# Joining three edits in a two-block fp32 transformer kernel: latent-attention keys and rotations, the norms of block 2, and the RG-LRU gelu

## The chip, the cores and the metric

The kernel runs on one core of a Trainium2 chip, as one program and one launch. The metric is the device time of an execution in microseconds (us), lower is better; the number to forecast is the median of several executions. TensorE is called PE here, its weight loads PEld, VectorE DVE, ScalarE ACT, GpSimd POOL, and SyncE SP.

## The reference

512 tokens of width 1024 in fp32 go through two blocks of two layers each. A layer of block 1 joins three attention branches (latent attention "MLA", a dilated one, a neighbourhood one) by gates and adds a SwiGLU part. Block 2 has a retention layer and an RG-LRU layer, each followed by a SwiGLU part, with a norm before and after each part:

```python
for layer in range(DEPTH):                       # block 2
    h = rms_norm_2(x, norm_g[layer, 0])
    m = retention_mixer(...) or rglru_mixer(...)
    x = x + rms_norm_2(m, norm_g[layer, 1])
    f = swiglu_ffn(rms_norm_2(x, norm_g[layer, 2]), ...)
    x = x + rms_norm_2(f, norm_g[layer, 3])
...
# rglru_mixer
y_branch, u = jnp.split(x @ w_in, 2, axis=-1)
y_branch = jax.nn.gelu(y_branch, approximate=True)
u = conv4(u) + conv_b
r, i = sigmoid(u_blocks @ gate_w + gate_b)       # 6 blocks of 256
log_a = -LRU_C * r * softplus(-a_param)
b = sqrt(-expm1(2 * log_a)) * (i * u)
h = associative_scan(a, b)
return (h * y_branch) @ w_out
```

## The kernel before

**Products.** Activations lie transposed, 128 features by 512 tokens a tile. Each fp32 operand is split into a high part that PE takes in fast (fp32r) and a low remainder: `zh, zl` for activations, `wh, wl` for weights. A 128x128 tile of weights against a tile of activations is three matmuls of 512 columns: `wh*zh, wh*zl, wl*zh`. In the trace such a step is the rows `zh,wh`, `zl,wh`, `zh,wl`.

**Weights.** All weights lie in one tensor in the order in which PE takes them, in chunks of eight tiles. SP loads a chunk into `raw` (two buffers), ACT copies it to `wh`, DVE subtracts to `wl` (a ring of three each), and both count as "the split". Where in its own work ACT or DVE splits the next chunk is decided by `reach(mark, n)` (up to chunk n after a named point), by `ahead()`, or by a wait that needs that chunk.

**Order.** There is no scheduler: every engine's program is written out by hand, and `wait_ge`/`tell` tie them with semaphores. `claim(bank, ...)` makes PE wait until the last user of one of the eight PSUM banks has been moved out. In the attention parts PE takes units (one head's 128 queries each): transposes, scores, value products, and then some "fill" steps of other products, as many as `SLOTS` say.

**MLA (`tensor_mla`, `vector_mla`, ...).** 32 units. A unit's chain is: PE scores, DVE minimum (L1248), ACT exp, DVE reciprocal (L1088), POOL division `m_p` (L578), PE transpose, ACT and DVE split `m_pth, m_ptl`. The query of the next head is turned on DVE (`m_qf`), then split on ACT (`m_qh`) and POOL (`m_ql`). The rotations of the dilated part's first heads run in between: shuffle and sine on DVE, cosine (`b_qk<-b_qk,b_rc`) on POOL.

**Dilated and neighbourhood parts.** `b_bank`, `BV_BANK`, `gate_bank`, `proj_bank`, `c_bank` give the bank of each fill; `FILL_N` is the order of the fills in the neighbourhood part: gate g and projection p of 8 column tiles, query q and key k of the last head pairs. Gates of odd number and all q lie in bank 1. DVE moves a fill out in the unit after the one in which it ended.

**After each part of block 2 (`*_post`).** `ret`, `f20`, `lru` and `f21` are the four posts. Eight output tiles come (the last in two halves of 256 tokens), their squares are summed over features by one-column matmuls (`tensor_half`), POOL takes the root, PE spreads it over the partitions, DVE scales `mb`, DVE or POOL adds it to `x2`, and then the next part's `zh` (ACT) and `zl` (DVE) are made by halves. PE begins the next part with three tiles by halves (`halves`). The squares of the new x for its norm are ACT's, 16 of 256 tokens, and each is summed by PE with one-column matmuls (`bank<-small,mb`): after each of the eight second-half steps (`early`) and after four steps of the next tile (`late`). `f21` has no next part.

**RG-LRU (`*_lru`).** Six blocks b of two tiles: PE takes the gates' matmuls of block b and then the input products of block b+2; ACT, DVE and POOL run the recurrence, and `u_hyh, u_hyl` (`scalar_hy`, `vector_hy`) are the operands of the output product. After the gates of block 4, PE goes to output tiles 0 to 3 over inputs 0 to 7. The gelu: ACT squares `u_y` into `u_q`, ACT scales and biases it, POOL multiplies by `u_y`, ACT takes tanh, DVE multiplies.

## Time and profile before

| | us |
|---|---|
| median of 3 executions (3360.37 to 3360.75) | 3360.4 |
| the profiled execution's own time | 3354.7 |
| its span, first to last instruction | 3352.9 |
| PE busy | 3282.0 (98%) |
| DVE, ACT, POOL busy | 1783.3, 1318.1, 604.8 |

PE is busy nearly throughout, so only time in which PE waits, works at half clock, or does work that could be left out can be won. The time of a matmul in a row is longer than its spacing to the next one, since they overlap; spacings are read from the starts.

### The profile page before, as it was taken

The page shows a single profiled execution, that of the slowest core. Times are in us where ns is not written, and L with a number is a line of the kernel's source. Part 1 is how long each engine was busy: PE and PEld are TensorE (multiplying, and loading weights), DVE is VectorE, ACT ScalarE, POOL GpSimd, SP SyncE. Part 2 cuts the span into 40 slices and gives each one's busy share as a digit, 9 for nine tenths or more (in the row PEclk, how much of TensorE's full clock was granted, in tenths as well). Part 3 has the DMA queues.
Part 4 walks back from the last instruction along what each step waited for, and adds up shares of the span by engine and source line. Part 5 has one row for each costly group of instructions (what it writes and reads, how often), then busy time and mean ns, then how long its engine had stood idle before and what let it go on. Part 6 is the DMA issues. An engine that isn't in the chain of part 4 may idle for free.

```text
span 3352.9 us, 38507 instructions
## 1 busy us (share of the span) xinstructions
PE 3282.0 (98%) x15604; PEld 2722.5 (81%) x15604; DVE 1783.3 (53%) x2671; ACT 1318.1 (39%) x2025; POOL 604.8 (18%) x516
## 2 busy tenths in 40 slices
PE   8999999999999999999999999999999999999998
PEld 7787878888887887788888888888888888788887
DVE  6764565444447655755444455544444359854433
ACT  5643453333236534533332323333232248733321
POOL 1420122011003310320110021111111025521101
PEclk9999999999999999999999999999999999999999
DMA  3022223222321122222323222222232222223232
GB/s 133 32 70 76 96 90 107 95 95 94 100 90 57 58 71 78 98 95 94 101 94 105 94 79 81 90 88 76 95 100 95 98 73 88 95 65 106 96 99 82
DMA packets 84993, 295.61 MB, mean 88 GB/s; under 512 B 9424, under 2 KB 11984, under 8 KB 84816
## 3 DMA queue, kind: packets, MB, share of 16 engines
q1 hardware_dynamic: 84816, 293.15, 26.4%
q8 instruction: 123, 2.02, 0.2%
q14 instruction: 54, 0.44, 0.0%
HBM read 291.02 MB, written 2.10 MB: 87 GB/s over the span
## 4 chain that ended last, share of the span: by engine, by line
PE 83%; DVE 8%; ACT 4%; issue 2%; POOL 2%; DMA 1%; SPq 0%; POOLq 0%; DVEq 0%; ACTq 0%
PE bank L312 81%; PE bank L315 2%; DVE wl L555 2%; ACT wh L528 1%; DVE small L1248 1%; POOL u_g L575 1%; DVE u_uc L551 1%; DMA raw<-in_wts 1%; DVE m_ptl L555 1%; POOL u_q L575 0%; DVE u_h L3123 0%; ACT c_k L528 0%; ACT b_v L528 0%; POOL x L575 0%; DVE m_qf L545 0%
## 5 line engine op out<-in xcount | busy, mean ns | idle before, releaser
L555 DVE TENSOR_TENSOR wl<-raw,wh 128x1024 fp32r<-128x1024 f32 (+1 forms) x531 | 682.2, 1288 | 860.4 <-ACT wh L528 859.4
L312 PE MATMUL bank<-zh,wh 128*128 128x512 f32 (+1 forms) x2652 | 1034.3, 390 | 14.7 <-ACT zh L528 7.7
L312 PE MATMUL bank<-zl,wh 128*128 128x512 f32 (+1 forms) x2652 | 1022.7, 386 | 5.5 <-DVE zl L558 5.4
L312 PE MATMUL bank<-zh,wl 128*128 128x512 f32 (+1 forms) x2652 | 1023.2, 386 | 4.0 <-DVE wl L555 4.0
L528 ACT ACTIVATE wh<-raw 128x1024 fp32r<-128x1024 f32 (+1 forms) x531 | 556.4, 1051 | 537.8 <-PE bank L312 477.3
L312 PEld LDWEIGHTS bank<-zh,wh 128*128 128x128 f32 x2652 | 502.1, 189 | 116.0 <-ACT zh L528 8.0
L312 PEld LDWEIGHTS bank<-zh,wl 128*128 128x128 f32 x2652 | 501.8, 189 | 109.1 <-DVE wl L555 8.3
L312 PEld LDWEIGHTS bank<-zl,wh 128*128 128x128 f32 x2652 | 502.1, 189 | 102.3 <-DVE zl L558 7.6
L312 PE MATMUL bank<-f_mh,wl 128*128 128x512 f32 (+1 forms) x748 | 283.7, 379 | 1.2 <-DVE wl L555 1.2
L312 PE MATMUL bank<-f_mh,wh 128*128 128x512 f32 (+1 forms) x748 | 284.1, 380 | 0.0
L312 PE MATMUL bank<-f_ml,wh 128*128 128x512 f32 (+1 forms) x748 | 281.4, 376 | 0.0
L575 POOL TENSOR_TENSOR f_t<-f_t 128x512 f32<-128x512 f32 x88 | 113.6, 1291 | 792.6 <-DVE f_t L551 792.6
L581 POOL TENSOR_TENSOR small<-small 128x1 f32<-128x1 f32 (+3 forms) x35 | 44.3, 1265 | 965.5 <-DVE small L548 965.5
L531 ACT ACTIVATE f_t<-f_t 128x512 f32<-128x512 f32 x88 | 55.6, 632 | 293.4 <-DVE f_t L545 293.3
L312 PEld LDWEIGHTS bank<-f_mh,wl 128*128 128x128 f32 x748 | 140.4, 188 | 29.6 <-DVE wl L555 1.6
L312 PEld LDWEIGHTS bank<-f_ml,wh 128*128 128x128 f32 x748 | 140.4, 188 | 28.1
L312 PEld LDWEIGHTS bank<-f_mh,wh 128*128 128x128 f32 x748 | 140.6, 188 | 25.4
L312 PE MATMUL bank<-wh,zh 128*128 128x512 f32 (+2 forms) x384 | 145.0, 378 | 0.7 <-ACT r_r L528 0.7
L312 PE MATMUL bank<-wl,zh 128*128 128x512 f32 (+2 forms) x384 | 143.7, 374 | 1.5 <-DVE wl L555 1.5
L528 ACT ACTIVATE f_mh<-f_t 128x512 fp32r<-128x512 f32 x88 | 55.6, 632 | 227.3 <-POOL f_t L575 227.3
L312 PE MATMUL bank<-wh,zl 128*128 128x512 f32 (+2 forms) x384 | 143.9, 375 | 0.0
L545 DVE TENSOR_TENSOR f_t<-bank,rrow 128x512 f32<-128x512 f32 x88 | 60.8, 691 | 141.3 <-PE bank L312 130.6
(336 smaller groups left out, 4483.4 us busy)
## 6 DMA issues: line engine op xcount, KB each, us to landing
...
```

Source lines behind the costliest of these rows:

```text
L312: return self.e.matmul(out, l, r, start=start, stop=stop, skip_group_check=inside)
L315: return self.e.transpose(out, in_, self.m.ident)
L528: return self.e.activation(out, in_, ACT.Copy, scale=scale)
L531: return self.e.activation(out, in_, func, **kw)
L545: return self.e.tensor_tensor(out, a, b, op)
L551: return self.e.scalar_tensor_tensor(out, a, s, b, op0, op1)
L555: return self.e.tensor_tensor(out, src, b32(hi), ALU.subtract)
L575: return self.e.tensor_tensor(out, a, b, op)
L581: return self.e.tensor_tensor(out, v, self.m.negh[:, 0:n], ALU.pow)
L1248: L.e.tensor_reduce(m.mn[:, c:c + 1], m.bank[4 + i % 2], AX.X, ALU.min).then_inc(*L.tell("mn", "mla", l, i))
```

## The change

It joins edits in several places. (1) MLA: the cosine product of the six early rotations goes from POOL to DVE; each head's query is turned one unit sooner; the low parts of the values (`m_v`) are made in units 0 and 1, no longer ahead of unit 0. (2) Dilated part: the fills take banks 2, 1, 0, 1, 0, 1 and no longer 0, 1, 0, 1, 0, 1; DVE moves a projection out after the reciprocal and no longer ahead of it. (3) Neighbourhood part: the fills q3 and k3 come ahead of g2 and p2. (4) Posts: the squares for the next norm are 8 of 512 tokens at the end, DVE adds them up, and PE sums over features once, with four one-column matmuls, three tiles later; the second half of the last output tile has bank 4; scaled rows come at k = 6; splits are placed by `reach`. (5) RG-LRU: the gelu's middle is one DVE instruction in place of ACT's and POOL's; output tiles 0 to 3 take inputs 0 to 5 and then 6 and 7; `hy` of blocks 3 and 5 comes sooner; one `reach` ahead of the rows.

```diff
-BV_BANK = ((3, 4, 5, 6), (2, 1, 3, 0))
+BV_BANK = ((3, 4, 5, 6), (2, 1, 0, 3))
...
-    return (2, 7)[w] if p == 0 and g == 0 else w if p else 0
+    if p:
+        return (2, 1, 0, 1, 0, 1)[2 * g + w]
+    return 0 if g else (2, 7)[w]
...
+    if p == 0:
+        x = m.b_qk[p][2 * g + w]
+        L.tt(x, x, m.b_rc, ALU.mult).then_inc(*L.tell("ev", "cos", *n))
...
-    L.wait_ge("pl", *n)
+    if p == 0:
+        L.wait_ge("ev", "cos", *n)
+    else:
+        L.wait_ge("pl", *n)
...
+def vector_mv(L, l, t):
+    m = L.m
     vv = m.m_v.rearrange("p (t h d) -> p t h d", t=4, h=8)
-    for t in range(4):
-        L.wait_ge("hi", "mv", l, t)
-        L.lo(vv[:, t, :, 64:128], m.bank[V_BANK[t]].rearrange("p (h d) -> p h d", h=8), vv[:, t, :, 0:64]).then_inc(
-            *L.tell("lo", "mv", l, t))
-    L.ahead()
+    L.wait_ge("hi", "mv", l, t)
+    L.lo(vv[:, t, :, 64:128], m.bank[V_BANK[t]].rearrange("p (h d) -> p h d", h=8), vv[:, t, :, 0:64]).then_inc(
+        *L.tell("lo", "mv", l, t))
...
@@ scalar_mla, vector_mla, gpsimd_mla
-        if i % 4 == 2 and i < 30:
+        if i % 4 == 1 and i < 29:
             scalar_q(L, l, i // 4 + 1)
...
+        if i < 2:
+            vector_mv(L, l, 2 * i)
+            vector_mv(L, l, 2 * i + 1)
...
-        if i in B_TURN:
-            gpsimd_b(L, ("b", l, 0) + B_TURN[i])
...
-                yield from L.steps(n, 8, L.z_whole(), b_desc, w, ("cp",) + n)
+                yield from L.steps(n, 8, L.z_whole(), b_desc, b_bank(n), ("cp",) + n)
...
@@ vector_dil
             if x == "g":
                 vector_gate(L, l, 0, n)
-            else:
-                vector_proj(L, l, 0, n)
...
             vector_div(L, i, *key)
+        for x, n in at(p, i, 1) if p else ():
+            if x == "p":
+                vector_proj(L, l, 0, n)
...
-FILL_N = bb(0) + [("q", 2), ("k", 2)] + bb(1, 2) + [("q", 3), ("k", 3)] + bb(3, 4, 5, 6, 7)
+FILL_N = bb(0) + [("q", 2), ("k", 2)] + bb(1) + [("q", 3), ("k", 3)] + bb(2, 3, 4, 5, 6, 7)
...
-POST_BANK = {"ret": (0, 1, 2, 3, 4, 5, 0, 2, 3), "f20": (2, 3, 6, 7, 4, 5, 0, 1, 2), "f21": (2, 3, 6, 7, 4, 5, 0, 1, 2),
-             "lru": (4, 5, 6, 7, 0, 1, 2, 3, 2)}
+POST_BANK = {"ret": (0, 1, 2, 3, 4, 5, 0, 2, 4), "f20": (2, 3, 6, 7, 4, 5, 0, 1, 4), "f21": (2, 3, 6, 7, 4, 5, 0, 1, 4),
+             "lru": (4, 5, 6, 7, 0, 1, 2, 3, 4)}
 POST_SCALE = {"ret": 1.0, "f20": 1.0, "f21": 1.0, "lru": -0.125}
-POST_AT = {"ret": 0, "f20": 3, "f21": 3, "lru": 0}
-POST_ROWS = {"ret": 7, "f20": 9, "f21": 9, "lru": 7}
+POST_AT = {"ret": 1, "f20": 3, "f21": 3, "lru": 0}
+POST_ROWS = 6
+
+POST_EARLY = {"ret": 1, "f20": 0, "lru": 1}
...
-    sb, rb = ((6, 7), (4, 5))[h]
+    sb, rb = 6, (7, 5)[h]
...
@@ scalar_post
+    if nxt:
+        L.reach(("z2", s), POST_EARLY[s])
     for h in range(2):
         for n in range(8):
             if nxt:
-                g = m.col(nxt)
                 L.wait_ge(*x_ready(s, n, h, False))
-                L.cp(half(m.zh[n], h), half(m.x2[n], h), g[:, n:n + 1]).then_inc(*L.tell("zh", "z2", s, n, h))
-                L.fn(half(m.mb[n], h), half(m.x2[n], h), ACT.Square).then_inc(*L.tell("cp", "xsq", s, n, h))
+                L.cp(half(m.zh[n], h), half(m.x2[n], h), m.col(nxt)[:, n:n + 1]).then_inc(*L.tell("zh", "z2", s, n, h))
             if h == 0 and n == POST_AT[s]:
                 scalar_m7(L, s, 1)
                 if nxt:
                     L.reach(("z2", s), 1)
-            if nxt and h == 0 and n == POST_AT[s] + 3:
+            if nxt and h == 0 and n == POST_AT[s] + 2:
                 L.reach(("z2", s), 2)
-            if h:
-                L.ahead()
+            if nxt and h and n == 6:
+                L.reach(("z2", s), 3)
+    for n in range(8 if nxt else 0):
+        L.fn(m.mb[n], m.x2[n], ACT.Square).then_inc(*L.tell("cp", "xsq", s, n))
+        if n == 3:
+            L.reach(("z2", s), 4)
...
@@ vector_post
-        L.ts(m.mb[n], m.bank[POST_BANK[s][n]], g[:, n:n + 1], POST_SCALE[s], ALU.mult, ALU.mult).then_inc(
-            *L.tell("ev", "m", s, n))
         if n:
             if n > 1:
                 L.wait_ge("sq", "m", s, n - 1)
             L.tt(m.sqa, m.sqa, m.sqt, ALU.add).then_inc(*L.tell("sq", "m", s, n))
+        L.ts(m.mb[n], m.bank[POST_BANK[s][n]], g[:, n:n + 1], POST_SCALE[s], ALU.mult, ALU.mult).then_inc(
+            *L.tell("ev", "m", s, n))
...
+            if nxt and h == 0 and n == 2:
+                L.reach(("z2", s), POST_EARLY[s])
+            if h == 0 and n == POST_AT[s] + 2:
                 vector_m7(L, s, g, 1)
-            if h == 0 and n == POST_AT[s] + 2:
                 if nxt:
                     L.reach(("z2", s), 1)
+            if h == 0 and n == POST_AT[s] + 3:
...
+    if nxt:
+        L.reach(("z2", s), 3)
+    for n in range(1, 8 if nxt else 0):
+        if n > 1:
+            L.wait_ge("sq", "x", s, n - 1)
+        else:
+            L.wait_ge("cp", "xsq", s, 0)
+        L.wait_ge("cp", "xsq", s, n)
+        L.tt(m.mb[0], m.mb[0], m.mb[n], ALU.add).then_inc(*L.tell("sq", "x", s, n))
+        if n == 4:
+            L.reach(("z2", s), 4)
...
@@ tensor_next_stat
-    def squares(h, ns):
-        def go():
-            ps = L.claim(6, "rv", *N) if (h, ns[0]) == (0, 0) else m.bank[6]
-            for n in ns:
-                L.wait_ge("cp", "xsq", s, n, h)
-                for r in (2 * h, 2 * h + 1):
-                    new = (h, n, r) == (0, 0, 0)
-                    t = L.mm(ps[:, r:r + 1], m.mb[n][:, 128 * r:128 * r + 128], m.ones, new, new or n == 7, not new)
-            if (h, ns[-1]) == (1, 7):
-                t.then_inc(*L.tell("st", "stat", *N))
-        return go
-
-    return ({(1, k): squares(0, (k,)) for k in range(8)}, {k: squares(1, (2 * k, 2 * k + 1)) for k in range(4)}, L.spread(N))
+    def squares():
+        ps = L.claim(6, "rv", *N)
+        L.wait_ge("sq", "x", s, 7)
+        L.sums(ps, 0, m.mb[0], True).then_inc(*L.tell("st", "stat", *N))
+
+    return squares, L.spread(N)
...
@@ tensor_ffn2
-             {(0, 0): squares1, (0, 3): rows1, **early})
+             {(0, 0): squares1, (0, 4): rows1})
     n = F + (1, 1)
-    L.group([n], 8, L.z_whole(), f2_in_desc, [3], [("ev",) + n], late)
+    L.group([n], 8, L.z_whole(), f2_in_desc, [3], [("ev",) + n])
     for i in range(2, FF):
         n = [F + (w, i) for w in range(2)]
         L.group(n, 8, L.z_whole(), f2_in_desc, [f_bank(i, w) for w in range(2)], [("ev",) + x for x in n],
-                {1: rows} if i == 2 else {})
+                {0: squares, 2: rows} if i == 2 else {})
...
@@ tensor_lru
-    pair(y[0:2], y_bank, {1: rows})
+    pair(y[0:2], y_bank, {0: squares, 2: rows})
...
-            for i in (0, 2):
-                tensor_post_pair(L, "lru", i, LW, x, lru_out_desc, range(8))
+            for ks in (range(6), range(6, 8)):
+                for i in (0, 2):
+                    tensor_post_pair(L, "lru", i, LW, x, lru_out_desc, ks)
...
-    q = m.u_q[n % 2]
-    L.fn(q, m.u_y[n % 4], ACT.Square).then_inc(*L.tell("cp", "y2", n))
+    L.fn(m.u_q[n % 2], m.u_y[n % 4], ACT.Square).then_inc(*L.tell("cp", "y2", n))
+
+
+def vector_y_cube(L, n):
+    q, v = L.m.u_q[n % 2], L.m.u_y[n % 4]
     L.wait_ge("cp", "y2", n)
-    L.fn(q, q, ACT.Identity, scale=0.044715 * 0.7978845608028654, bias=m.gel).then_inc(*L.tell("cp", "y3", n))
-
-
-def gpsimd_gelu(L, n):
-    q, v = L.m.u_q[n % 2], L.m.u_y[n % 4]
-    L.wait_ge("cp", "y3", n)
-    L.tt(q, q, v, ALU.mult).then_inc(*L.tell("pl", "y3", n))
+    L.stt(q, q, 1.0 / 0.044715, v, ALU.add, ALU.mult).then_inc(*L.tell("ev", "y3", n))
 
 
 def scalar_gelu(L, n):
     q = L.m.u_q[n % 2]
-    L.wait_ge("pl", "y3", n)
-    L.fn(q, q, ACT.Tanh).then_inc(*L.tell("th", "y", n))
+    L.wait_ge("ev", "y3", n)
+    L.fn(q, q, ACT.Tanh, scale=0.044715 * 0.7978845608028654).then_inc(*L.tell("th", "y", n))
...
@@ scalar_lru
+    L.reach(("z2", "f20"), 7)
...
+        if b in (4, 6):
+            scalar_hy(L, b - 1)
         if b < 6:
             scalar_recur(L, b)
+        for n in nxt:
+            scalar_y_square(L, n)
         lru_reach(L, b, 1)
-        if b:
+        if b in (1, 2, 3, 5):
             scalar_hy(L, b - 1)
         for n in nxt:
             scalar_us(L, n)
-        lru_reach(L, b, 2)
-        for n in nxt:
-            scalar_y_square(L, n)
...
@@ vector_lru
+        if b in (4, 6):
+            vector_hy(L, b - 1)
...
+        if b == 5:
+            vector_hy(L, b - 1)
+        for n in nxt:
+            vector_y_cube(L, n)
...
```

Three places in the order of the instructions follow. PE, after the retention part: the last step of the second half of the first three tiles (256 columns), and the steps that follow (bank 3 is the fourth tile, `mb0` to `mb7` the squares of x). Before:

```order
L312 MATMUL bank2<-zh,wl1 128x256
L312 MATMUL bank6<-small,mb7 128x1 x2
L312 MATMUL bank3<-zh,wh2 128x512
L312 MATMUL bank3<-zl,wh2 128x512
L312 MATMUL bank3<-zh,wl2 128x512
L312 MATMUL bank6<-small,mb0 128x1 x2
L312 MATMUL bank6<-small,mb1 128x1 x2
```

And of the changed kernel, where the only such rows stand, one tile later (banks 4 and 5 are the third pair of tiles):

```order
L312 MATMUL bank4<-zh,wl0 128x512
L312 MATMUL bank5<-zh,wh0 128x512
L312 MATMUL bank5<-zl,wh0 128x512
L312 MATMUL bank5<-zh,wl0 128x512
L312 MATMUL bank6<-small,mb0 128x1 x4
L312 MATMUL bank4<-zh,wh0 128x512
```

Thirty-two one-column matmuls of a post have become four, and they come after one step of the third pair.

PE, neighbourhood part of layer 0, unit 5: scores, then the last two steps of projection 1 (`ybh, ybl`, bank 0), then the next fill. Before:

```order
L312 MATMUL bank5<-c_kl1,c_q10 128x256
L312 MATMUL bank0<-ybh,wh2 128x512
L312 MATMUL bank0<-ybl,wh2 128x512
L312 MATMUL bank0<-ybh,wl2 128x512
L312 MATMUL bank0<-ybh,wh2 128x512
L312 MATMUL bank0<-ybl,wh2 128x512
L312 MATMUL bank0<-ybh,wl2 128x512
L312 MATMUL bank2<-zh,wh2 128x512
```

Of the changed kernel, from the same place:

```order
L312 MATMUL bank0<-ybh,wh2 128x512
L312 MATMUL bank0<-ybl,wh2 128x512
L312 MATMUL bank0<-ybh,wl2 128x512
L312 MATMUL bank1<-zh,wh2 128x512
L312 MATMUL bank1<-zl,wh2 128x512
```

The fill behind the projection was gate 2 in bank 2 and is now q3 in bank 1, where gate 1 ended at the end of unit 4.

DVE, RG-LRU, from the scan of block 3 to the third split (`u_h` is the scan, `u_y` the input of the gelu, `u_uc` the convolution). Before:

```order
L3123 SCALAR_TENSOR_TENSOR u_h<-u_t,u_g 128x512 x2
L555 TENSOR_TENSOR wl<-raw,wh 128x1024 x2
L545 TENSOR_TENSOR u_y<-bank,rrow 128x512 x2
L551 SCALAR_TENSOR_TENSOR u_uc<-u_pad,cols,u_uc 128x512 x6
L555 TENSOR_TENSOR u_hyl<-u_h,u_hyh 128x512 x2
L555 TENSOR_TENSOR u_usl<-u_uc,u_ush 128x512 x2
L551 SCALAR_TENSOR_TENSOR u_g<-u_g,u_uc 128x512 x2
L555 TENSOR_TENSOR wl<-raw,wh 128x1024
L551 SCALAR_TENSOR_TENSOR u_t<-u_t 128x512 x4
L555 TENSOR_TENSOR wl<-raw,wh 128x1024
```

Of the changed kernel:

```order
L3143 SCALAR_TENSOR_TENSOR u_h<-u_t,u_g 128x512 x2
L555 TENSOR_TENSOR wl<-raw,wh 128x1024 x2
L545 TENSOR_TENSOR u_y<-bank,rrow 128x512 x2
L555 TENSOR_TENSOR u_hyl<-u_h,u_hyh 128x512 x2
L551 SCALAR_TENSOR_TENSOR u_uc<-u_pad,cols,u_uc 128x512 x6
L555 TENSOR_TENSOR u_usl<-u_uc,u_ush 128x512 x2
L551 SCALAR_TENSOR_TENSOR u_g<-u_g,u_uc 128x512 x2
L555 TENSOR_TENSOR wl<-raw,wh 128x1024
L551 SCALAR_TENSOR_TENSOR u_t<-u_t 128x512 x4
L551 SCALAR_TENSOR_TENSOR u_q<-u_q,u_y 128x512 x2
L555 TENSOR_TENSOR wl<-raw,wh 128x1024
```

`u_hyl` now stands ahead of the convolution, the third split stays behind both, and the cube `u_q<-u_q,u_y` is new.

## Rows read from the trace of the kernel before

**Rows 1.** Waits of PE, whole run: us in total, times, longest.

```profile
PE bank L315 <- POOL m_p L578: 7.5, 10, 1.0
...
PE bank L312 <- DVE u_hyl L555: 5.4, 1, 5.4
PE bank L312 <- DVE zl L558: 5.4, 6, 1.6
PE bank L312 <- DVE m_qf L545: 4.8, 8, 1.4
PE bank L312 <- DVE b_v L558: 3.0, 2, 1.6
PE bank L312 <- DVE c_kl L555: 3.0, 2, 1.5
PE bank L312 <- ACT wh L528: 2.9, 2, 1.5
...
PE bank L312 <- POOL m_ql L575: 2.3, 2, 1.2
PE bank L315 <- POOL b_p L578: 2.3, 2, 1.1
...
PE bank L312 <- DVE mb L548: 2.0, 1, 2.0
```

**Rows 2.** Instructions on tile mb, PE: ns min/median/max, first and last start.

```profile
L312 PE MATMUL bank<-small,mb x192: 164/250/250, 2340.6 to 2997.8; 128*128 128x1 f32 x192
```

**Rows 3.** Timeline of PE behind the retention post: start us, us, instruction.

```profile
2339.54 0.28 PE L312 MATMUL bank<-zh,wh 128*128 128x256 f32 x1
...
2340.62 0.50 PE L312 MATMUL bank<-small,mb 128*128 128x1 f32 x4
...
2342.13 0.50 PE L312 MATMUL bank<-small,mb 128*128 128x1 f32 x4
...
2352.34 0.95 PE L312 MATMUL bank<-small,mb 128*128 128x1 f32 x8
...
2353.48 0.40 PE L312 MATMUL bank<-zl,wh 128*128 128x512 f32 x1
2353.71 0.39 PE L312 MATMUL bank<-zh,wl 128*128 128x512 f32 x1
2353.95 0.95 PE L312 MATMUL bank<-small,mb 128*128 128x1 f32 x8
```

**Rows 4.** Timeline of DVE in the retention post; brackets: idle before, releaser.

```profile
2324.59 0.48 DVE L548 TENSOR_SCALAR mb<-bank,cols 128x256 f32<-128x256 f32 x1 [2.06 <-ACT rrow L531]
...
2325.32 0.48 DVE L558 SCALAR_TENSOR_TENSOR zl<-x,cols,zh 128x256 fp32r<-128x256 f32 x1
```

**Rows 5.** Windows at half clock: length, busy (count) by engine, granted clock, DMA.

```profile
184.20:187.70 3.50, 3.50 (x10) 2.71 (x10) 2.33 (x5) 0.89 (x2) 0.00 (x0) 0.51 0.22 62
2327.80:2334.70 6.90, 5.89 (x26) 5.32 (x26) 5.26 (x12) 3.23 (x7) 3.98 (x5) 0.51 0.37 122
2891.00:2897.90 6.90, 4.81 (x11) 3.80 (x12) 6.90 (x12) 4.69 (x7) 2.50 (x1) 0.51 0.00 0
```

**Rows 6.** Timeline of DVE in RG-LRU block 4.

```profile
2892.36 1.28 DVE L555 TENSOR_TENSOR u_hyl<-u_h,u_hyh 128x512 fp32r<-128x512 f32 x2
...
2895.97 1.21 DVE L555 TENSOR_TENSOR wl<-raw,wh 128x1024 fp32r<-128x1024 f32 x1
```

**Rows 7.** Timelines of POOL and DVE in RG-LRU block 1.

```profile
2807.22 7.73 POOL L575 TENSOR_TENSOR u_q<-u_q,u_y 128x512 f32<-128x512 f32 x2 [10.36 <-ACT u_q L531]
...
2815.05 1.70 DVE L551 SCALAR_TENSOR_TENSOR u_y<-u_q,u_y 128x512 f32<-128x512 f32 x1 [1.30 <-ACT u_q L531]
```

**Rows 8.** Timeline of POOL in MLA.

```profile
78.48 1.80 POOL L575 TENSOR_TENSOR b_qk<-b_qk,b_rc 128x512 f32<-128x512 f32 x1 [0.56 <-DVE m_sh L783]
```

**Rows 9.** Timelines of PE and DVE, neighbourhood part, unit 5, layer 0.

```profile
413.64 0.39 PE L312 MATMUL bank<-zh,wh 128*128 128x512 f32 x1
...
416.30 0.67 DVE L545 TENSOR_TENSOR f_g<-bank,rrow 128x512 f32<-128x512 f32 x1
```

More of the change, by code:

```diff
@@ L1256, in vector_mla @@
             L.lo(lo, f4(m.bank[turn_bank(j)]), hi).then_inc(*L.tell("lo", "pt", "mla", l, j))
-        if i % 4 == 2 and i < 30:
+        if i % 4 == 1 and i < 29:
             vector_q_turn(L, l, i // 4 + 1)
@@ L1276, in gpsimd_mla @@
             gpsimd_div(L, i - 1, m.m_p[(i - 1) % 4], "mla", l)
-        if i % 4 == 2 and i < 30:
+        if i % 4 == 1 and i < 29:
             gpsimd_q(L, l, i // 4 + 1)
-        if i in B_TURN:
-            gpsimd_b(L, ("b", l, 0) + B_TURN[i])
         if i >= 16 and i % 8 == 0:
@@ L2647, in tensor_post @@
     L.halves([("m", s, 7)], K, (by_half(x[0]), by_half(x[1])), desc, [[POST_BANK[s][7]], [POST_BANK[s][8]]],
-             [[("ev", "m7", s, h)] for h in range(2)], {(1, 2): squares, (1, POST_ROWS[s]): rows}, False)
+             [[("ev", "m7", s, h)] for h in range(2)], {(1, 2): squares, (1, POST_ROWS): rows}, False)
     L.end(("post", s), "pe")
@@ L2725, in stat @@
         L.wait_ge("st", "half", s, h)
-        L.ts(m.vtmp[:, c], m.bank[(6, 4)[h]][:, c], 1.0 / 1024, EPS, ALU.mult, ALU.add).then_inc(*L.tell("rv", "half", s, h))
+        L.ts(m.vtmp[:, c], m.bank[6][:, c], 1.0 / 1024, EPS, ALU.mult, ALU.add).then_inc(*L.tell("rv", "half", s, h))
     def z(n, h):
@@ L2745, in vector_post @@
                 z(n - 2, h)
-            if h == 0 and n == POST_AT[s] + 1:
+            if nxt and h == 0 and n == 2:
+                L.reach(("z2", s), POST_EARLY[s])
+            if h == 0 and n == POST_AT[s] + 2:
                 vector_m7(L, s, g, 1)
-            if h == 0 and n == POST_AT[s] + 2:
                 if nxt:
                     L.reach(("z2", s), 1)
+            if h == 0 and n == POST_AT[s] + 3:
                 stat(1)
@@ L2753, in vector_post @@
                 L.reach(("z2", s), 2)
-            if h:
-                L.ahead()
         if nxt:
@@ L2774, in gpsimd_post @@
                 L.tt(half(m.x2[n], h), half(m.x2[n], h), half(m.mb[n], h), ALU.add).then_inc(*L.tell("pl", "x", s, n, h))
-            if h == 0 and n == POST_AT[s] + 2:
+            if h == 0 and n == POST_AT[s] + 3:
                 rms(1)
@@ L2814, in tensor_ffn2 @@
     squares1, rows1 = tensor_half(L, prev, 1)
-    early, late, rows = tensor_next_stat(L, prev)
+    squares, rows = tensor_next_stat(L, prev)
     first = [F + wi for wi in ((0, 0), (1, 0), (0, 1))]
@@ L2899, in tensor_lru @@
     y = [("y", i) for i in range(LW)]
-    early, late, rows = tensor_next_stat(L, prev)
+    squares, rows = tensor_next_stat(L, prev)
     L.skip()
@@ L2903, in tensor_lru @@
     L.halves(u[:3], 8, L.z_by_half("z2", prev), lru_desc, [range(3)] * 2, [[("ev",) + n for n in u[:3]]] * 2,
-             {(0, 0): squares1, (0, 3): rows1, **early})
-    L.group(u[3:4], 8, L.z_whole(), lru_desc, [3], [("ev", "u", 3)], late)
+             {(0, 0): squares1, (0, 4): rows1})
+    L.group(u[3:4], 8, L.z_whole(), lru_desc, [3], [("ev", "u", 3)])
     def pair(ns, bank, extra={}):
         L.group(ns, 8, L.z_whole(), lru_desc, [bank(n[1]) for n in ns], [("ev",) + n for n in ns], extra)
-    pair(y[0:2], y_bank, {1: rows})
+    pair(y[0:2], y_bank, {0: squares, 2: rows})
     pair(y[2:4], y_bank)
@@ L3215, in vector_lru @@
     L.wait_ge("ev", "pads")
+    L.reach(("z2", "f20"), 7)
     L.wait_ge("rr", "z2", "f20")
@@ L3229, in vector_lru @@
     for n in range(2):
+        vector_y_cube(L, n)
+    for n in range(2):
         vector_gelu(L, n)
@@ L3240, in vector_lru @@
         lru_reach(L, b, 1)
-        if b:
+        if 0 < b < 4:
             vector_hy(L, b - 1)
@@ L3249, in vector_lru @@
             vector_recur(L, b)
+        if b == 5:
+            vector_hy(L, b - 1)
+        for n in nxt:
+            vector_y_cube(L, n)
         lru_reach(L, b, 3)
@@ L3262, in gpsimd_lru @@
     gpsimd_stat(L, ("z2", "f20"))
-    for n in range(2):
-        gpsimd_gelu(L, n)
     for b in range(7):
@@ L3267, in gpsimd_lru @@
             gpsimd_hv(L, b - 1)
-        if b < 5:
-            for n in (2 * b + 2, 2 * b + 3):
-                gpsimd_gelu(L, n)
         if b < 6:
```

## The prediction

> **What bounds the kernel now.** I began with the table of busy times. PE is busy 3282.0 of 3352.9 us, every other engine far less: a stretch is shorter only if PE has less to do, waits less, or works less at half clock. So I took the waits of PE [rows 1]. The reader is to see that no wait dominates: the longest are single ones (5.4 us for `u_hyl` in the RG-LRU), and most are families of ten waits of a microsecond, which recur in both layers of block 1 (`m_p`, `m_qf`, `b_v`). The ten rows sum to 38.6 us. Next I looked for work of PE that does not multiply weights: the one-column matmuls on `mb` [rows 2] and their spacing [rows 3]. Last the windows at half clock [rows 5]: in each the granted clock is 0.51, that is 1.2 GHz where 2.4 is granted elsewhere, and each stands right behind waits of PE.
>
> **The sum, part by part.** Each price is PE time.
>
> *1. Squares of the posts.* A second-half step is nine matmuls of 256 columns: from 2339.54 to 2340.62 they take 1.08 us. With a squares group between, the spacing of two groups is 2342.13 - 2340.62 = 1.51 us, so four short records cost 0.43 us. A late group: 2353.95 - 2352.34 = 1.61 us for eight records and three matmuls of 512 columns spaced 0.23 (2353.48 to 2353.71), 0.69 us: 0.92 us for eight records [rows 3]. A post has eight early and four late groups, 3.4 + 3.7 = 7.1 us. 192 records on three posts [rows 2] become 24, one group of eight a post, 0.92 us. Gain (7.1 - 0.9) x 3 = **18.6 us**. The Trainium skill ("TensorE: Matmul & The Clock Gate", section Back-to-back issue gap) gives about 60 cycles for a lone matmul of 1 to 64 columns, 25 ns at 2.4 GHz; by it 168 records would be worth 4.2 us. The rows show 0.11 us a record, and they decide.
>  What takes the squares' place lies off PE: ACT's squares are 8 of 512 for 16 of 256, DVE gets seven additions of 512 elements (0.67 us each by `f_g` [rows 9], 4.7 us), and both can lie under the fourth tile and the first step of the third pair (5.5 + 1.4 us of PE at 0.23 a matmul), which start when the second halves are done. Without that cover each late microsecond is one of PE, three times. POOL's root has two steps (2.7 us) until PE wants its rows: I cost it at nothing, 0 to 1 us a post.
>
> *2. Waits and clock in the posts.* In the retention post DVE stood 2.06 us for the second half of the last tile (`rrow`), with the first `zl` queued behind it [rows 4]: that move now stands two tiles later, so the first 1.6 us wait on `zl` should go. ACT without its 16 squares feeds `zh` sooner, which is for the other `zl` waits. The bank of the second half of the last tile is now one emptied first: the 2.0 us on `mb` goes. The first split after `f20` is now stated ahead: half of ACT `wh`'s 2.9, 1.5 us. Together 5.4 + 2.0 + 1.5 = 8.9 [rows 1]; since some waits will only shrink, **8 us** (bounds 2 and 8.9). The window at 2327.80 holds 26 matmuls in 6.90 us at 0.51 [rows 5]. Its wait for `zl` apart, 26 matmuls spaced 0.12 would be 3.1 us, so the clock costs about 2 there. Behind the RG-LRU post PE works the same way, and I put it at the same: **4 us** together (0 to 5).
>
> *3. RG-LRU.* PE waits 5.4 us for `u_hyl` of block 3, behind twelve tiles of the output product; released at 2893.0 when the first `u_hyl` ends [rows 6]. Now twelve tiles of pair 2, 3 come first, 12 x 0.69 = 8.3 us: the wait is covered. What is late next: the split behind. PE would want its `wl` at 2887.6 + 8.3 + 0.5 = 2896.4; it ended at 2895.97 + 1.21 = 2897.2 [rows 6], and ACT's two squares (1.2 us) now stand ahead of `u_ush`: about 2898.5. A new wait of 2 to 2.5 us. The half clock behind the old wait (11 matmuls in 4.81 us busy [rows 5], 2.5 at 0.23) gives 2.2 back. 5.4 + 2.2 - 2.5 = **5.1 us** (1 to 7.6). Splits ahead of the rows at the start: the other half of ACT `wh`, **1.4 us**.
>  The gelu: DVE gets 12 cubes, 0.67 us each by `f_g` again, two a block. I cost them at nothing, because DVE stood 1.30 us before the first gelu multiply for ACT's tanh [rows 7]; with the cover gone they are 8.0 us. POOL loses `u_q`, of which two took 7.73 us [rows 7], while DVE ran on. The Trainium skill ("SBUF — State Buffer", section Who interferes with whom) says that a DVE instruction with two SBUF inputs and a POOL instruction that reads SBUF exclude each other; the cubes have two such inputs, so POOL's later products may have to wait behind them as `u_q` did. No row prices this for the new order.
>
> *4. MLA.* `b_qk` on POOL takes 1.80 us [rows 8], and the next `m_p` stands behind it. Six times a layer this goes; DVE's cosine in its place delays the next minimum by 0.67, so I count half of the 7.5 us of `m_p`, 3.7. Queries one unit sooner should end nearly all of `m_qf` 4.8 and `m_ql` 2.3 [rows 1]; 5.8. Sum **9.5 us** (0 to 14.6). The values' low parts move from ahead of the first minimum to units 0 and 1: four DVE instructions of 512 elements that are wanted only by the first value product in unit 6; the cover is the fill work of PE.
>
> *5. Dilated part.* The first fill has bank 2, emptied first, not bank 0 emptied last: 3.0 us of `b_v` [rows 1], and the spell at 184.20, 10 matmuls in 3.50 us for 2.3 at 0.23, but with the last begun before its end: 1.6 us a time, two layers 3.2. **6.2 us** (3.0 to 6.2). The projection behind the reciprocal: `b_p`, **2.3 us** (0 to 2.3; the projection's bank is free 0.7 us later, under eight steps of gate).
>
> *6. Neighbourhood part.* q3 and k3 ten steps sooner end `c_kl`, +3.0 us [rows 1]. But q3 claims bank 1, where gate 1 ended in the unit before, with two steps of projection between. The next fill starts at 413.64; DVE moves gate 1 out (`f_g`) from 416.30 to 416.97 [rows 9]. Behind q3 PE's scores of unit 6 are queued, and DVE and ACT for them. New wait 3.3 us, two layers: -6.7. Sum **-3.7 us** (+3.0 to -10 with half clock behind it).
>
> Sum: 18.6 + 8 + 4 + 5.1 + 1.4 + 9.5 + 6.2 + 2.3 - 3.7 = 51.4 us. The profiled execution goes from 3354.7 to 3303.3, its span from 3352.9 to 3301.5; the median of the runs is 5.7 above the profiled one, and I keep that: 3360.4 - 51.4 = **3309.0**.
>
> **Rivals.**
> *DVE becomes what is waited for.* It gets 12 cosines, 12 cubes and 21 additions, 45 x 0.67 = 30 us. For: in MLA it is already in the chain of each unit. Against: it is 53% busy over the run. Then MLA gives nothing, the cubes cost 5, and the posts' waits give 3 of 8: 51.4 - 9.5 - 5 - 5 = 32 us, 3328.
> *All waits named go, and q3 finds its bank empty.* For: the order of DVE could shift by what the other edits free. Against: the rows of unit 5. 51.4 + 6.7 + 5 (the rest of MLA) + 2.5 = 66 us, 3295.
> *The short matmuls cost little.* The 0.43 and 0.92 us could be change-over that the remaining order has anyway. Then part 1 is worth 4.2: 37 us, 3323. Against it: 0.43 us for four and 0.92 for eight are in proportion to the number of records, not of change-overs [rows 3]. The section of the Trainium skill named in part 1 would have it so.
> *Slower.* Mechanism: a wait of 3.3 us in the neighbourhood part or the split in the RG-LRU brings a long stretch at half clock. In the first window a matmul takes 0.35 us and more for 0.23, a loss of up to 1.6 us in 3.5 [rows 5]; to turn 51 us of gain into a loss of 0.2% (6.7) it takes 58 us, some 120 us at half clock. Against: the spells are 3.5 to 6.9 us long, the one behind the wait of 5.4 us too [rows 5]. It ends at 3368.
> *No change.* The gains do not add because one chain through DVE sets the time; little speaks for it at 98% PE.
>
> **How the numbers follow.** Forecast 0.46; DVE 0.26; all waits go 0.21; short matmuls 0.03; slower 0.02; no change 0.02. The range reaches from the case of all waits gone (3295) to that of DVE (3328) and, since costs in both layers and three posts repeat, some 7 us further: 3296 to 3335. Outside lie the last two cases and about half of a further tenth on each side. A change of 0.2% (6.7 us) is about what a measurement of this kernel tells from none: faster 0.96, same 0.02, slower 0.02.
>
> **What the changed profile would show.** Right: 24 records of `bank<-small,mb`; no early groups, second-half steps spaced 1.08; no waits on `b_v`, `u_hyl`, `mb`, `c_kl`; a wait of PE for `f_g` of some 3 us in each neighbourhood part; a wait for `wl` of 2 to 2.5 us in the RG-LRU output product; fewer half-clock spells in the posts; `m_p` waits of 0.5. Wrong would be: waits of PE on `mb<-mb` sums or on the root's rows of more than 1 us a post, minima of MLA starting later against PE than now, or a family of new `wl` waits in the RG-LRU because the cubes hold the splits back.

## The result, and the profile after

| | before | after |
|---|---|---|
| median of the executions, us | 3360.6 | 3325.1 (3324.4 to 3325.5, 4 runs) |
| profiled execution, own time | 3354.7 | 3324.4 |
| span | 3352.9 | 3322.6 |
| PE busy | 3282.0 | 3257.8 |
| DVE, ACT, POOL busy | 1783.3, 1318.1, 604.8 | 1805.0, 1309.0, 561.5 |

The ratio is 0.9894 (95% interval 0.9877 to 0.9911): faster by 35 us, where 51 were forecast. The sum of the steps was made for the profiled execution, and there the gain is 30.4 us. The other 5 us are a spread of the kernel before: its times went from 3353.0 to 3362.5 us over all its executions, and the one that I read was short. (One execution of a version below, that with 64 records a post, took 4653 us at a mean granted clock of 0.65, and stands in no ratio.)

The waits of PE in the changed kernel (us in total, times, longest), beside [rows 1]:

```profile
PE bank L315 <- POOL m_p L578: 13.2, 16, 2.1
...
PE bank L312 <- DVE f_g L545: 6.3, 2, 3.1
PE bank L315 <- POOL b_p L578: 5.2, 2, 2.6
PE bank L312 <- DVE wl L555: 4.6, 6, 1.5
PE bank L315 <- DVE c_ptl L555: 3.5, 2, 1.7
PE bank L312 <- DVE zl L558: 2.9, 2, 2.1
PE bank L312 <- DVE acc L551: 2.5, 2, 1.3
PE bank L312 <- DVE m_yf L545: 2.4, 2, 1.2
...
PE bank L312 <- DVE b_v L558: 0.7, 2, 0.4
...
PE bank L312 <- DVE u_hyl L555: 0.7, 1, 0.7
```

The reader is to see two things. What was named as going did go: `m_qf`, `m_ql`, `c_kl`, `mb` and ACT `wh` are not in the list, `b_v` and `u_hyl` nearly so. And block 1 has new ones in their place: `m_p` 5.7 us more, `f_g` 6.3, `b_p` 2.9 more, `c_ptl` 3.5, `acc` 2.5, `m_yf` 1.8 more.

Apart from the records on `mb` PE takes the same steps in both kernels, so the times at which the same step starts in the two timelines give a balance by stretch (us, to some 0.2; plus is a loss):

| stretch | forecast | measured |
|---|---|---|
| MLA, layers 0 and 1 | -9.5 | -0.1, +1.8 |
| dilated part | -8.5 | +1.3, +0.4 |
| neighbourhood part | +3.7 | +2.4, +3.8 |
| three posts, splits at the RG-LRU's start included | -32.0 | -10.9, -11.6, -9.4 |
| RG-LRU up to the end of its output product | -5.1 | -8.6 |
| the rest | 0 | +0.6 |
| sum | -51.4 | -30.3 |

Block 2 gave 40.5 us where 37.1 were forecast. Block 1, which was to give 14.3, took 9.6. The windows at half clock (length, PE's work and that of the others, granted clock, DMA), beside [rows 5]:

```profile
79.50:82.90 3.40, 3.40 (x12) 2.71 (x11) 3.37 (x7) 1.18 (x4) 0.69 (x1) 0.50 0.00 0
192.10:195.50 3.40, 3.40 (x10) 2.54 (x10) 1.98 (x7) 2.21 (x4) 0.91 (x1) 0.50 0.00 0
...
2943.30:2950.10 6.80, 6.80 (x34) 6.80 (x33) 4.99 (x11) 2.04 (x4) 5.47 (x6) 0.50 0.32 117
```

The first stands behind a wait of 2.07 us on `m_p`, the second behind 2.61 us on `b_p`. There are six of 3.4 us in block 1 and this one in block 2; before there were 10 us in block 1 and 20 in block 2. The last 7 to 8 us of a run, which are at half clock in every version, are left out here and below.

### The profile page after: what moved, and what is told of

Read it like the earlier page. It is cut to its first block, busy times and chain, and to the rows that moved or that the text cites. A ratio compares the mean times of both kernels' runs of the same rounds, so it can differ in the third digit from the quotient of the medians.

```text
span 3322.6 us, 38212 instructions
## 1 busy us (share of the span) xinstructions
PE 3257.8 (98%) x15436; PEld 2702.9 (81%) x15436; DVE 1805.0 (54%) x2716; ACT 1309.0 (39%) x1989; POOL 561.5 (17%) x492
## 4 chain that ended last, share of the span: by engine, by line
PE 83%; DVE 8%; ACT 3%; issue 2%; POOL 2%; DMA 1%; SPq 0%; POOLq 0%; DVEq 0%; ACTq 0%
PE bank L312 82%; PE bank L315 2%; DVE wl L555 1%; ACT wh L528 1%; DVE small L1258 1%; POOL u_g L575 1%; DMA raw<-in_wts 1%; ACT c_k L528 1%; DVE m_ptl L555 1%; DVE u_uc L551 0%; DVE m_qf L545 0%; DVE c_kf L545 0%; DVE u_t L551 0%; DVE b_yf L545 0%; DVE c_ptl L555 0%
```

## The experiments

Spans come from one profiled execution each. The windows at half clock move between executions of like kernels (some 13 to 41 us of them in a run, 58 in the one with 64 records, with about half of that lost), so a difference of under 3 us in a span says little; a wait by its name, or a stretch between two steps of PE, says more. Versions that were measured together share the runs of the kernel before, whose median was 3360.6 us beside the changed kernel and 3356.2 to 3358.8 beside the others; so the ratios compare better than the medians.

| run | span | median | ratio to before (95%) |
|---|---|---|---|
| changed kernel | 3322.6 | 3325.1 | 0.9894 (0.9877 to 0.9911) |
| block 2 alone | 3311.1 | 3310.8 | 0.9865 (0.9849 to 0.9881) |
| gate 1 in bank 2 | 3313.1 | 3313.0 | 0.9872 (0.9857 to 0.9887) |
| cosine on POOL | 3321.2 | 3320.1 | 0.9892 (0.9878 to 0.9907) |
| queries late | 3325.3 | 3327.8 | 0.9918 (0.9903 to 0.9933) |
| values' low parts first | 3319.3 | 3322.4 | 0.9896 (0.9881 to 0.9910) |
| dilated banks of before | 3321.3 | 3322.8 | 0.9895 (0.9881 to 0.9910) |
| gelu of before | 3329.9 | 3331.8 | 0.9925 (0.9910 to 0.9940) |
| 64 records a post | 3354.8 | 3359.4 | 1.0003 (0.9993 to 1.0013) |
| output order of before | 3318.5 | 3320.9 | 0.9896 (0.9879 to 0.9912) |
| joined | 3303.6 | 3306.8 | 0.9851 (0.9836 to 0.9866) |
| joined, low parts first | 3303.5 | 3303.4 | 0.9842 (0.9827 to 0.9856) |
| and `wl` later | 3297.0 | 3298.4 | 0.9818 (0.9804 to 0.9831) |

**Block 2 alone.** All edits of MLA, dilated and neighbourhood part taken out, that is parts (1) to (3) of the change.

> The changed kernel with every edit of block 1 taken out (MLA, dilated and neighbourhood part as in the kernel before); block 2 stays changed. Theory A (the two traces laid side by side by PE's steps: block 1 of the changed kernel ends 10.3 to 10.5 us later than before, block 2 takes 40.7 us less): the profiled span is 3352.9 - 40.7 = 3312, some 10 us under the changed kernel's 3322.6, with the waits m_qf 4.8, m_qf's neighbours and b_v 3.0 back and none on f_g. Rival B (the 10 us are a chance of the one execution, or block 2 gains only because block 1 shifted its splits and transfers): the span stays within 3 us of 3322.6.

Span 3311.1, 11.5 us below the changed kernel, and the waits of block 1 are those of before, but for a third one of 1.0 us on `b_p`:

```profile
PE bank L315 <- POOL m_p L578: 7.4, 10, 1.1
PE bank L312 <- DVE m_qf L545: 4.7, 8, 1.4
...
PE bank L312 <- DVE b_v L558: 3.1, 2, 1.7
PE bank L312 <- DVE c_kl L555: 3.0, 2, 1.5
```

So the edits of block 1 together cost what the balance says, and block 2's gain doesn't lean on them.

**Gate 1 in another bank.**

```diff
 def gate_bank(br, i):
-    return (..., (2, 1)[i % 2], (2, 0)[i % 2])[br]
+    return (..., 2 if i < 2 else (2, 1)[i % 2], (2, 0)[i % 2])[br]
```

> The changed kernel; gate 1 of the neighbourhood part goes to bank 2 in place of bank 1, so that q3 finds bank 1 empty. Nothing else. Theory A (q3 waits for the bank, 3.3 and 3.1 us): PE's wait on f_g (6.3 us in 2) is gone, the neighbourhood parts are 3 us shorter each, the span 3316. Rival B (DVE is late there for another reason, and the wait only takes another name): a wait of 2 us or more on c_kl, c_ptl or c_qf stands in its place and the span stays above 3320.

The wait on `f_g` is gone, and nothing stands in its place: `c_ptl` is 3.4 us, as it was. By the starts of PE's steps the two neighbourhood parts are 3.3 us shorter each at this place. The place in the changed kernel, DVE and then PE (brackets: idle before, releaser), beside [rows 9]:

```profile
414.67 1.23 DVE L555 TENSOR_TENSOR wl<-raw,wh 128x1024 fp32r<-128x1024 f32 x1 [2.74 <-ACT wh L528]
...
417.57 0.68 DVE L555 TENSOR_TENSOR c_ptl<-bank,c_pth 128x512 fp32r<-128x512 f32 x1
418.17 0.67 DVE L545 TENSOR_TENSOR f_g<-bank,rrow 128x512 f32<-128x512 f32 x1
...
418.90 0.50 PE L312 MATMUL bank<-zh,wh 128*128 128x512 f32 x1 [3.14 <-DVE f_g L545]
```

PE begins q3 as soon as gate 1 has been moved out. The whole span fell by 9.5 us: the 6.6, and a window at half clock less behind the second of these waits (1.7 us), the rest elsewhere.

**Three edits of MLA, each undone by itself.** The cosine on POOL:

```diff
+        if i in B_TURN:
+            gpsimd_b(L, ("b", l, 0) + B_TURN[i])
```

(in `gpsimd_mla`, and without the product in `vector_b_shift`.)

> The changed kernel with the cosine product of the six early rotations a layer back on POOL. Theory A (MLA's gain was eaten because work went to DVE, which is late for the minimum): m_p's waits of 13.2 us fall by some 3 us, MLA is 1 to 2 us a layer shorter than in the changed kernel. Rival B (POOL's 1.8 us ahead of the division cost as much as I had counted before the change): m_p's waits rise by 2 to 4 us.

`m_p` fell from 13.2 to 10.6 us and `m_yf` from 2.4 to 0.6: 4.4 us of waits less, so A. By the starts of PE's steps MLA is 2.5 us shorter in each layer, with as many windows at half clock in it. The whole span shows 1.4 of them; this execution had 34 us of half clock in block 1, where the changed kernel's had 20.

The queries a unit later:

```diff
-        if i % 4 == 1 and i < 29:
+        if i % 4 == 2 and i < 30:
```

(in the programs of ACT, DVE and POOL.)

> The changed kernel with each head's query turned one unit later, as before. Theory A (the query now stands in the same unit of DVE as the sum m_yf and the odd keys, so the next minimum is late): the m_p waits in front of units 4k+2 (1.07 and 1.02 us in layer 0) shrink by 0.6 each, but m_qf's waits of 4.8 us are back: net 0 to +3 us on the span. Rival B (the query's place is the whole cause of the m_p waits): m_p falls by 5 us or more and the span by 2 us.

`m_qf` is back with 7.9 us and `m_ql` with 2.3, `m_kal` has 1.0, and `m_p` fell from 13.2 to 6.8: 11.2 us of waits came and 6.4 went. MLA is 3.7 us longer by the starts of its steps, and the span rose by 2.7. Each theory has half of it. As B said, the queries' place makes the whole rise of `m_p` (5.7 us over before); as A said, it is a gain all the same, of some 4 to 5 us.

The low parts of the values first (`vector_mv` for t = 0 to 3 ahead of unit 0, and not in units 0 and 1).

> The changed kernel with the four low parts of the values ahead of unit 0 of MLA again, as before. Theory A (they stand between the minima of units 1 and 2 and make them late: PE's new wait of 2.07 us on m_p at 78.0): that wait falls below 1 us in both layers, ACT m_p's waits of 1 us at unit 0 come back (1.8 us), m_p in all from 13.2 to about 10, net -1 to -2 us. Rival B (they filled idle time of DVE and the 2.07 us have another cause): m_p's waits stay at 12 us or more and the span grows by 1 to 2.

`m_p` 11.0 and ACT `m_p` 1.9: 12.9 against 13.2, no gain beyond what the clock blurs. PE in this version, and below it in the changed kernel:

```profile
76.92 0.66 PE L315 MATMUL bank<-ident,m_p 128*128 128x128 f32 x4 [0.52 <-POOL m_p L578]
...
89.97 0.63 PE L315 MATMUL bank<-ident,m_p 128*128 128x128 f32 x4 [2.10 <-POOL m_p L578]
```

```profile
78.02 0.66 PE L315 MATMUL bank<-ident,m_p 128*128 128x128 f32 x4 [2.07 <-POOL m_p L578]
...
91.06 0.63 PE L315 MATMUL bank<-ident,m_p 128*128 128x128 f32 x4 [0.90 <-POOL m_p L578]
```

The wait at 78.02 fell to 0.52 us, as A said; but the long wait came back, from the first unit in which a query is turned to the second, and so `m_p` fell by 2.2 us only, 1.9 of them given back on ACT `m_p`. The low parts are at most the occasion of the long wait, not its cause. Neither theory has the span: it fell by 3.3 us, with 7 us less at half clock.

**Banks of the dilated part as before** (`BV_BANK`, `b_bank`, and the fills' banks w).

> The changed kernel with the banks of the dilated part's fills as before. Theory A (PE's wait for b_v, 3.0 us, didn't go away: it moved to the first b_p, 5.2 us now, since DVE is as late as it was): b_v's 3 us are back, b_p falls to 1 or 2 us, and the dilated parts take the same time within 1 us a layer. Rival B (the banks won their 3 us, and b_p's wait has a cause of its own): b_v back, b_p still near 5 us, span +2 to +3.

`b_v` is back with 3.9 us and `b_p`'s 5.2 are gone from the list. PE's waits from 180 to 200 us, in the changed kernel and then with the old banks:

```profile
PE bank L315 <- POOL b_p L578: 2.6, 1, 2.6
PE bank L312 <- DVE b_v L558: 0.3, 1, 0.3
```

```profile
PE bank L312 <- DVE b_v L558: 2.0, 1, 2.0
```

This is A: `b_p` is ready when DVE's chain is, and PE, let past `b_v`, stands for it. The new banks even cost more waits than they end: 5.9 us on `b_v` and `b_p` together, against 3.9. By the starts of PE's steps the dilated part is 1.1 us longer with them in layer 0 and 0.2 shorter in layer 1, where the old banks have a window at half clock more.

**The gelu of before** (ACT scales, POOL multiplies; no cubes), everything else of the RG-LRU as changed.

> The changed kernel with the middle of the gelu as before: ACT scales and biases, POOL multiplies; the cubes are gone from DVE. Theory A (as predicted, the cubes cost and give nothing, the cover holds): the stretch of the RG-LRU up to the output product stays within 1 us, span within 1.5 us. Rival B (POOL, which took 3.9 us for a product beside DVE, held h and so u_hyl back, and part of the 8.6 us that the layer won comes from there): span +2 to +4, with a wait on u_hyl, u_usl or u_y back. Rival C (the cubes cost up to 8.0 us): the span falls by 3 or more.

Span +7.3, and the RG-LRU 9.0 us longer by the start of the same steps, one window at half clock of 3.4 us included. The waits of PE from 2740 us to the post, changed kernel and then this one:

```profile
PE bank L312 <- DVE wl L555: 1.0, 2, 0.5
PE bank L312 <- DVE u_hyl L555: 0.7, 1, 0.7
```

```profile
PE bank L312 <- DVE wl L555: 6.1, 5, 1.7
...
PE bank L312 <- ACT wh L528: 2.1, 1, 2.1
PE bank L312 <- DVE u_hyl L555: 0.7, 1, 0.7
```

Rival B has the sign, at twice its size, but by another way than it said: `u_hyl` is not late, the splits are, by 7.2 us of waits. ACT stands for POOL's product ahead of tanh (0.64 us at 2746.70), with the next `wh` behind it. And DVE's last product of the gelu is slow beside one of POOL's. In the changed kernel DVE has cube and product in a row, and here it is POOL that is slow:

```profile
2798.12 3.95 POOL L575 TENSOR_TENSOR u_g<-u_g,u_t 128x512 f32<-128x512 f32 x1 [14.09 <-DVE u_t L551]
2798.49 1.29 DVE L551 SCALAR_TENSOR_TENSOR u_q<-u_q,u_y 128x512 f32<-128x512 f32 x2
...
2802.03 1.29 DVE L551 SCALAR_TENSOR_TENSOR u_y<-u_q,u_y 128x512 f32<-128x512 f32 x2
2802.15 3.46 POOL L575 TENSOR_TENSOR u_g<-u_g 128x512 f32<-128x512 f32 x1
```

That is 0.69 us each on DVE, against 1.70 for `u_y` before [rows 7]; over the twelve, `u_y` has a median of 0.68 us now, 1.73 before and 1.48 in this version. POOL's two products beside them took 1.30 and 1.63 us before (from 2814.90), when DVE was the slow one. The section "Who interferes with whom" of the Trainium skill ("SBUF — State Buffer") says that such a DVE instruction and a POOL instruction that reads SBUF shut each other out, and the traces agree. So the meeting of the two has not gone, it has changed sides: POOL now takes longer; DVE's scan stands 5.9 us for it in all, and PE shows no new wait for either. What the edit gains is that no POOL product stands in the gelu's chain. How much of the 9 us comes from the chain and how much from DVE's shorter products no run tells apart.

The kernel before shows how much the other edits of the RG-LRU do by themselves. From the step at 2750 us of its trace to the post the changed kernel is 10.3 us shorter than it, and this version, with the old gelu, 1.3.

**Records in a row.** PE sums all eight squares of 512 tokens itself: 32 one-column matmuls a post, each of which stands in the trace as two records.

```diff
-        L.sums(ps, 0, m.mb[0], True)
+        for n in range(8):
+            for r in range(4):
+                t = L.mm(ps[:, r:r + 1], m.mb[n][:, 128 * r:128 * r + 128], m.ones, ...)
```

> The changed kernel; PE sums all eight squares of 512 tokens over the features itself, with 64 records in place of 8 a post, at the same place, and DVE's 21 additions are gone. That is 168 records more on three posts, as many as the change removed, but in a row. Theory A (0.11 us a record, as I read from the spacings before): span +18.5 us, 6.2 a post. Rival B (about 25 ns each, the rest of the spacing was change-over between kinds of matmul): +4.2 us, 1.4 a post.

The span grew by 32.2 us, more than by either theory. The records of the retention post (length, PE and PEld busy with their counts, the others, granted clock):

```profile
2360.30:2363.90 3.60, 3.59 (x33) 3.59 (x33) 0.00 (x0) 0.00 (x0) 0.00 (x0) 1.00 0.17 66
2363.90:2370.54 6.64, 6.64 (x33) 6.64 (x32) 0.00 (x0) 0.00 (x0) 0.00 (x0) 0.50 0.00 0
```

At full clock 33 records take 3.60 us, 0.109 each, with PEld busy throughout; then the clock is halved and they take 0.201. So A's price holds (168 x 0.109 = 18.3 us), and B is refuted: in a row there is no change-over. What neither theory had is the clock: in each post PE runs at 1.2 GHz for 10 to 14 us from within the records on, 34 us in all by the windows, where the changed kernel has 6.8 in its posts. Half of the 27 us between them is the other 14. The Trainium skill ("TensorE: Matmul & The Clock Gate", Back-to-back issue gap) gives about 60 cycles for a matmul of 1 to 64 columns by itself, and says of such lone figures that they leave the weight load out. These fp32 records each load weights of their own, and 0.109 us is over four times the 25 ns that I had taken from the page.

**The output product's order as before** (`range(8)` in place of `range(6)` and `range(6, 8)`).

> The changed kernel with PE's order of the RG-LRU output product as before: tiles 0 to 3 over inputs 0 to 7, pair by pair. Theory A (two edits did it together: u_hyl of block 3 is now ready at 2873.5 to 2874.1, 10 us after the product's start, where it was 15 us before, and the order covers only the rest): a wait of 1.3 to 2 us on u_hyl, span +1 to +2.5. Rival B (the order alone ended the wait of 5.4 us): the wait is back at 4 us or more with a window of half clock behind it, span +5 to +8.

The waits in the product:

```profile
PE bank L312 <- DVE u_hyl L555: 1.3, 1, 1.3
PE bank L312 <- DVE u_usl L555: 1.0, 1, 1.0
```

That is 2.3 us, against 1.6 there in the changed kernel (`u_hyl` 0.7, `wl` 0.5, `u_usl` 0.4), and the stretch up to the post took no longer. The span is 4.1 us shorter by chance of the clock: no window at half clock fell into the RG-LRU post (2.1 us), and 1.5 us come from ahead of block 2, where the two kernels are alike. So A has the wait right, B is refuted, and the order itself is worth under 1 us. What ended the rest of the 5.4 us is `hy` placed sooner, by exclusion: with the gelu of before `u_hyl` of block 3 starts as soon, 7.6 us after the product's first step (2879.46 against 2871.84), but no run has `hy` alone at its old place. `u_hyl` of block 3 now starts at 2872.83, 9.0 us after the product's first step at 2863.83, where it was 13.9 us before (2892.36 [rows 6] against 2878.46).

**A version from these runs.** The changed kernel with gate 1 in bank 2, the cosine on POOL and the old banks of the dilated part; then with the low parts first as well.

> A version from what the runs showed: the changed kernel with the cosine back on POOL, gate 1 of the neighbourhood part in bank 2, and the dilated part's banks as before; the queries stay one unit sooner, the values' low parts in units 0 and 1. Theory A (the waits of the parts add up): 3322.6 - 6.3 (f_g) - 4.2 (m_p 2.6 and m_yf 1.8) - 2 (b_v and b_p together) - 2 to 4 of half clock less = 3306 to 3308. Rival B (DVE stays late, each wait taken away comes back under another name, as when the values' low parts were moved): no faster than 3311, the span of the version that has none of block 1's edits.

> As the version before it, and the values' low parts ahead of unit 0. Theory A (m_p's wait of 2.07 us behind them came back at the fourth unit only because the cosine stood on DVE there): with the cosine on POOL that wait is below 1.3 us, ACT m_p's 1.8 us are back, net -1 to +1 us against the version before it. Rival B: it comes back at 2 us, span 1.5 to 2 us above.

Spans 3303.6 and 3303.5. The first is even below A's range. By name some 11 us of waits went (6.3 on `f_g`, 2.1 on `b_v` and `b_p`, 1.8 on `m_yf`, but only 1.0 on `m_p`), and 10 us less at half clock give some 5 more. So the waits of separate parts do add up, and the last few us are the clock's. In the second `m_p` is 9.5 in place of 12.2, ACT `m_p` 1.8 is back, and the span is the same, as A said; but the longest `m_p` wait is 1.88 us, as B said. The place, DVE in the second version:

```profile
83.30 0.67 DVE L545 TENSOR_TENSOR m_qf<-bank,m_t 128x512 f32<-128x512 f32 x1
85.62 1.49 DVE L555 TENSOR_TENSOR wl<-raw,wh 128x1024 fp32r<-128x1024 f32 x1 [1.65 <-ACT wh L528]
87.03 0.68 DVE L1248 TENSOR_REDUCE small<-bank 128x1 f32<-128x512 f32 x1
```

DVE turns the query, then stands for ACT's `wh`, which stands behind ACT's `m_qh`, which waits for that same query; the minimum stands behind it all. The last run moved this split only:

```diff
-        L.ahead()
+        if i % 4 != 1 or i >= 29:
+            L.ahead()
```

(at the end of a unit of `vector_mla`.)

> As the last version, and DVE's split at the end of the units 4k+1 of MLA, those in which the query is turned, stands behind the next unit's minimum and reciprocal (three places a layer). There DVE stood 1.65 us for ACT's wh, which stood behind m_qh, and then took 1.49 us for wl, with the minimum behind it (85.62 to 87.03 of the last version's trace), and PE's longest wait on m_p, 1.88 us, came at 88.7. Theory A (the split ahead of the minimum makes these m_p waits): the three waits of a layer, 0.5, 1.9 and 0.7 us, shrink to under 0.5 each, m_p falls from 9.5 to 5 us or less, span 3303.5 - 5 = 3298 to 3300. Rival B (DVE simply has too much work there, and what isn't late at one unit is late at the next): m_p stays at 8 us or more, or waits on wl of 2 us or more come in their place, span within 1.5 us of 3303.5.

DVE at the same place of this version, and PE's waits:

```profile
81.67 0.67 DVE L545 TENSOR_TENSOR m_qf<-bank,m_t 128x512 f32<-128x512 f32 x1
82.26 0.67 DVE L1248 TENSOR_REDUCE small<-bank 128x1 f32<-128x512 f32 x1
82.86 0.15 DVE L1088 RECIPROCAL small<-small 128x1 f32<-128x1 f32 x1
83.98 1.48 DVE L555 TENSOR_TENSOR wl<-raw,wh 128x1024 fp32r<-128x1024 f32 x1 [0.98 <-ACT wh L528]
```

```profile
PE bank L315 <- POOL m_p L578: 4.3, 8, 1.3
PE bank L312 <- DVE wl L555: 4.1, 5, 1.5
```

`m_p` fell from 9.5 to 4.3 us with no new wait on `wl`: A. Some of it came back, 0.7 us on `m_ptl` and 0.9 more on `b_v`, and of the 6.5 us of span some 2 are a window less at half clock. This is the fastest version, 0.9818 of before, some 26 us below the changed kernel.

## Why the prediction was right, and where it was not

The direction and the range held. On the profiled execution the forecast was 21 us too good (3303.3 against 3324.4); 5 us of that are missing in the medians, because I carried the 5.7 us between profiled execution and median over, and the changed kernel has only 0.8. That the time stayed well within the range is in part luck: block 1 missed by 24 us, and the gelu, which the sum has at nothing, made up for some 9 of them. The measured 3325 lies nearer to the rival of DVE (3328) than to the forecast, and that rival has the reason right for MLA alone.

**1. Squares.** Right, in size too. There are 24 records. A group of eight with the three matmuls behind it takes 1.58 us (2360.54 to 2362.12), three such matmuls alone 0.68: 0.90 us for the group, against 0.92 forecast. The spacings of the early and late groups of before recur through the retention post, so a post gave 6.2 us and three 18.7, where I had 18.6. The run with 64 records shows the price of a record in a row of its own. That DVE's additions cost PE nothing holds too: there is no wait on `mb`, and that on `rrow` is 0.6 us in both kernels.

**2. Waits and clock in the posts.** Right. `zl` 2.5 us less, `mb` 2.0 less, ACT `wh` gone. Three posts gave 31.9 us together where steps 1 and 2 and the splits made 32.0. One family is missing in [rows 1] and in the sum: PE waited 7.2 us in ten for `wl`, and waits 4.6 in six now, 1.0 less in the posts. And the clock's share is partly chance: the posts have 6.8 us at half clock where they had 14, and in the run with the old output order none. One wait of 2.1 us on `zl` is left in the RG-LRU post, with a window of half clock behind it.

**3. RG-LRU.** Mis-sized term: the new wait on `wl`, 2 to 2.5 us, measured 0.5, with 0.7 on `u_hyl`. And the wrong term: the gelu, "I cost them at nothing". The gelu edit is worth 7 to 9 us in this kernel, since it takes POOL out of a chain of three engines; and the other edits of the RG-LRU with the splits at its start, which were to give 6.5, give 1.3 without it. So the total of this part (8.6 for 5.1) came near by luck. What I had named, that POOL's later products would have to wait behind the cubes, did come (3.95 us for one of `u_g`), but PE didn't wait for them.

**4. MLA.** The step that failed: "I count half of the 7.5 us of `m_p`" and "Queries one unit sooner should end nearly all of `m_qf` ... and `m_ql`; 5.8". The second came true and was paid back in `m_p` (+5.7); the 1.8 more on `m_yf` is the cosine's. I asked whether the work fits under PE's work, and not where it stands on DVE: ahead of the minimum, with a split behind a wait for ACT between them. The cosine is a loss of 4.4 us of waits, not a gain; the place of the values' low parts is worth nothing; the query sooner is a gain, but of some 4 to 5 us only; and the split behind it costs another 4 to 5, as the last run shows. Of my signs of being wrong, the minima of MLA later against PE came, and the `m_p` waits of up to 2.1 us with them, where I had 0.5. The rival "DVE becomes what is waited for" was right for MLA, wrong in its cubes (5 us lost) and in the posts (5 us lost).

**5. Dilated part.** Failed: "3.0 us of `b_v`" and "`b_p`, 2.3 us". PE passed `b_v` and waited for the first `b_p`, at the end of the same chain through DVE. With the projection behind the reciprocal the later `b_p` wait of 1.1 us went, and one on `acc` of 1.3 us came in each layer. That edit wasn't tried alone, so its part rests on the names of the waits.

**6. Neighbourhood part.** The new wait was right in place, cause and size: 6.3 us for 6.7. Its other side failed: "q3 and k3 ten steps sooner end `c_kl`, +3.0". `c_kl` and `c_qf` (1.0) went, and `c_ptl` came with 3.5, so the edit brought 0.5.

What stays open: where a window at half clock falls in an execution, which moves spans of like kernels by some us; and why the kernel before has executions 5 us apart.
